# Seven Strassen products for half of each MLP up-projection chunk, interleaved with the down-projection of another chunk

## The reference, cut to what matters

```python
def squared_relu_mlp(u, w1, w2):
    hdn = jnp.square(jax.nn.relu(jnp.einsum("bsd,df->bsf", u, w1)))   # 256x2048 by 2048x8192
    return jnp.einsum("bsf,fd->bsd", hdn, w2)                          # 256x8192 by 8192x2048

for i in range(DEPTH):                                                 # DEPTH = 2
    u = rmsnorm(h, norm_mix[i])
    m = conformer_conv_module(u, ...) if i % 2 == 0 else short_gated_conv(u, ...)
    h = h + m
    h = h + squared_relu_mlp(rmsnorm(h, norm_mlp[i]), mlp_w1[i], mlp_w2[i])
    h = h + per_layer_embedding(h, p[i], norm_ple[i], ple_w_proj[i], ple_w_gate[i])
return rmsnorm(h, norm_final)
```

## Time and profile before

| what | value |
|---|---|
| median of three runs | 2257.17 us |
| span of the profiled execution | 2255.2 us |
| PE busy | 2239.5 us, 99% of the span |
| DVE busy | 1429.0 us, 63% |
| ACT busy | 1145.0 us, 51% |
| granted TensorE clock, mean | 0.999 |
| DMA read / written | 460.42 / 33.55 MB, 219 GB/s over the span |

### The profile page before, as it was taken

The page is one execution under the profiler, slowest core; times in us unless marked ns, Lnnn a source line. Parts: engine busy times, 40 slices in busy tenths (PEclk is TensorE's granted clock), DMA queues, the critical chain, the costliest instruction groups (busy, mean ns, idle before and its releaser), DMA issues.

```text
span 2255.2 us, 29901 instructions
## 1 busy us (share of the span) xinstructions
PE 2239.5 (99%) x10320; PEld 1867.2 (83%) x10320; DVE 1429.0 (63%) x1597; ACT 1145.0 (51%) x1424; POOL 157.0 (7%) x183
## 2 busy tenths in 40 slices
PE   9999999999999999999999999999999999999998
PEld 8998788888888888888888888888888888888886
DVE  6999876555545645566766667665455455555665
ACT  5666655534534534556644444554345345345555
POOL 3888000000000000000000000000000000000000
PEclk9999999999999999999999999999999999999999
DMA  9554577756756856877777677777567567667773
GB/s 343 163 161 139 163 235 252 243 188 214 251 188 196 266 190 203 254 218 261 217 241 223 214 246 216 255 240 244 193 200 260 196 200 256 199 209 220 267 242 112
DMA packets 494098, 494.86 MB, mean 219 GB/s; under 512 B 257936, under 2 KB 296016, under 8 KB 493264
## 3 DMA queue, kind: packets, MB, share of 16 engines
q1 hardware_dynamic: 492192, 491.31, 67.6%
q10 hardware_dynamic: 1696, 1.67, 0.2%
q0 software_dynamic: 144, 1.05, 0.1%
HBM read 460.42 MB, written 33.55 MB: 219 GB/s over the span
## 4 chain that ended last, share of the span: by engine, by line
PE 98%; DMA 1%; DVE 1%; ACT 0%; issue 0%; ACTq 0%; SPq 0%; DVEq 0%
PE acc L430 29%; PE acc L432 29%; PE acc L431 29%; PE acc L494 3%; PE acc L513 2%; PE acc L515 2%; PE acc L514 2%; PE acc L548 1%; PE acc L578 0%; PE acc L577 0%; PE acc L576 0%; DMA emb<-in_cf_b_pw 0%; DMA staged<-prows 0%; ACTq L720 0%; DMA pT<-staged 0%
## 5 line engine op out<-in xcount | busy, mean ns | idle before, releaser
L939 DVE TENSOR_TENSOR wlo<-raw,whi 128x1024 fp32r<-128x1024 f32 x728 | 880.8, 1222 | 591.0 <-ACT whi L598 587.2
L598 ACT ACTIVATE whi<-raw 128x1024 fp32r<-128x1024 f32 x728 | 762.0, 1057 | 775.6 <-PE acc L432 769.9
L430 PE MATMUL acc<-whi,b_hi 128*128 128x512 f32 x1632 | 635.4, 389 | 0.0
L432 PE MATMUL acc<-whi,b_lo 128*128 128x512 f32 x1632 | 634.9, 389 | 0.0
L431 PE MATMUL acc<-wlo,b_hi 128*128 128x512 f32 x1632 | 634.9, 389 | 0.0
L430 PE MATMUL acc<-whi,a_hi 128*128 128x512 f32 x1280 | 498.1, 389 | 0.3 <-DVE a_lo L1034 0.3
L432 PE MATMUL acc<-whi,a_lo 128*128 128x512 f32 x1280 | 497.9, 389 | 0.0
L431 PE MATMUL acc<-wlo,a_hi 128*128 128x512 f32 x1280 | 497.9, 389 | 0.0
L431 PEld LDWEIGHTS acc<-wlo,b_hi 128*128 128x128 f32 x1632 | 306.3, 188 | 63.9 <-issue 0.2
L430 PEld LDWEIGHTS acc<-whi,b_hi 128*128 128x128 f32 x1632 | 306.3, 188 | 63.8 <-DVE b_lo L1256 0.3
L432 PEld LDWEIGHTS acc<-whi,b_lo 128*128 128x128 f32 x1632 | 306.3, 188 | 63.8
(11 more groups left out here) (169 smaller groups left out, 1256.4 us busy)
## 6 DMA issues: line engine op xcount, KB each, us to landing
raw<-in_mlp_w SPq DMA_DIRECT2D x256, 1024.0 KB, 5.8
raw<-in_sc_w_in SPq DMA_DIRECT2D x48, 1024.0 KB, 6.7
raw<-in_cf_w_pw SPq DMA_DIRECT2D x64, 512.0 KB, 8.8
raw<-in_ple_w_gate SPq DMA_DIRECT2D x32, 1024.0 KB, 6.7
staged<-prows SPq DMA_DIRECT2D x240, 128.0 KB, 3.3
pT<-staged SPq DMA_DIRECT2D x56, 512.0 KB, 3.3
raw<-in_cf_w_pw SPq DMA_DIRECT2D x16, 1024.0 KB, 7.3
raw<-in_sc_w_out SPq DMA_DIRECT2D x16, 1024.0 KB, 7.5
```

What stands on the lines that cost most here:

```text
L430: nc.tensor.matmul(o, xhi[:, k, s], hi, start=first and c == 0, stop=False)
L432: mm = nc.tensor.matmul(o, xlo[:, k, s], hi, start=False, stop=last and c == 1)
L598: nc.scalar.activation(whi[:, e % SLOTS, :, :], raw[:, e // 2, 2 * (e % 2):2 * (e % 2) + 2, :], ACT.Copy).then_inc(hi_ready, 1)
L939: nc.vector.tensor_tensor(wlo[:, e % SLOTS, :, :], raw[:, e // 2, 2 * (e % 2):2 * (e % 2) + 2, :], whi[:, e % SLOTS, :, :].bitcast(F32), A ...
```

## The change: what it does

Tokens, input rows and output columns of an up-projection are cut in two. Of the 2048 input rows, the first 1024 are computed by Strassen's scheme: the 256 tokens are two halves of 128, the 1024 rows two halves of 512, and 1024 output columns (a *chunk* of the hidden width, two result blocks) two halves of 512. Seven products of 128 tokens by 512 rows by 512 columns take the place of eight. The other 1024 input rows are multiplied as before. A layer has eight chunks. The first is computed as two blocks in the old way; for the seven others there is a *step*, which also does the down-projection of the chunk before it.

A step is a list of 38 *slots* (`STEP`), each with one split of 128x1024 weights on ACT and DVE: 14 slots `m` (two for each of the seven products, 6 matmuls each), 16 slots `d` (down-projection of the former chunk, four for each 512 output columns, 12 matmuls each), and 8 slots `r` (the other 1024 input rows, 12 matmuls each). Slots 0 to 25 are `m` and `d` mixed (slots 0, 1, 2 are `m`, slot 3 `d`, then `m` and `d` by turns to slot 17), 26 to 33 are `r`, 34 to 37 `d`. The first down-projection columns, `("d", 0, ...)`, stand in slots 3, 5, 7 and 9, and the latter two of these need the second result block of the former chunk. After seven steps `END` does the down-projection of the last chunk in 18 slots, of which the first four are half as large.

- Weights of the products need differences of blocks: `weight_sum` on DVE, 8 in a step, in place in `raw`, two slots ahead of their use. On the token side four combinations `s_hi`, `s_lo` are made once for each layer (`combine`).
- The partial sums are combined in PSUM by ACT (two copies, L1002 and L1005 of the new kernel) and DVE (`mix`, four operations, ahead of slot 18).
- `raw` holds the four 1 MB fields of the Strassen weights; all other weights of a step come as 24 loads of 512 KB into a ring of four, `pl`, each issued when the piece four loads earlier has been split.
- The embedding `emb` is written to DRAM in the first mixer's output projection and read back at the end of each MLP, to make room.
- The ring of split weights keeps four places; the semaphores are now `slot_hi`, `slot_lo`, `slot_used`, with PE's increment at the end of every slot.

The core of the diff (the parts for SP, PE, ACT and DVE in this order):

```diff
+STEP = (("m", 1, 0), ("m", 1, 1), ("m", 5, 0), ("d", 0, 0), ("m", 5, 1), ("d", 0, 1),
+        ("m", 6, 0), ("d", 0, 2), ("m", 6, 1), ("d", 0, 3), ("m", 7, 0), ("d", 1, 0), ("m", 7, 1), ("d", 1, 1),
...
+END = (("d", 0, 0, 0), ("d", 0, 0, 1), ("d", 0, 1, 0), ("d", 0, 1, 1), ("d", 0, 2, None), ("d", 0, 3, None),
...
+SUMS = (5, 6, 7, 4)
+SUMMED = tuple(i for i, (kind, of, _) in enumerate(STEP) if kind == "m" and of in SUMS)
+FIELD = {1: 0, 5: 0, 6: 0, 4: 0, 7: 1, 3: 2, 2: 3}
+COMBO = {5: 0, 6: 1, 7: 2, 3: 3}
+BANK = {1: 0, 2: 0, 7: 1, 4: 1, 5: 2, 3: 2, 6: 3}
...
+FIELD_FREED = (at_slot("m", 4, 1), at_slot("m", 7, 1), at_slot("m", 3, 1), at_slot("m", 4, 1))
+HIDDEN_BEFORE = tuple(last_up(c) + SLOTS for c in range(2))
...
+            def load_step(layer, k, last=False):
+
+                r0, r1 = (Result(chunk(layer, k), c) for c in range(2))
+                for i in range(len(STEP)):
+                    free = low_done(layer, k, i)
+                    if i in PLAIN:
+                        n = PLAIN.index(i) + 4
+                        if n < LOADS:
+                            plain(layer, k, n, free)
+                        elif last:
+                            plain_end(layer, n - LOADS, free)
+                        else:
+                            plain(layer, k + 1, n - LOADS, free)
+                    if i == HIDDEN_BEFORE[0] - 1:
+                        stage_begin(r0.T)
+                    if i == HIDDEN_BEFORE[0]:
+                        stage_end(r0.T)
+                    freed = [f for f in (3, 2, 1, 0) if i == FIELD_FREED[f]]
+                    for f in () if last else freed:
+                        field(layer, k + 1, f, free if f == freed[0] else None)
+                stage_begin(r1.T)
+                stage_end(r1.T)
...
+            def multiply_step(layer, u, k, parity, first=False):
+
+                hid, base, n = X[1 - u], first_slot(layer, k), STEPS * layer + k
+                up, _, down = mlp[layer]
+                before = Result(up, 0) if first else Result(chunk(layer, k - 1), 0)
...
+                        if of == 2:
+                            pe.wait_ge(m1_copied, n + 1)
+                        if of == 4:
+                            pe.wait_ge(mixed, n + 1)
...
+                    if kind == "d" and of == 0 and part % 2 == 0:
+                        pe.wait_ge(operand_ready, 2 * before.o + part + 2)
+                    pe.wait_ge(slot_lo, base + i + 1)
+                    for m in range(1 if kind == "m" else 2):
+                        for c in range(2):
+                            if kind == "m":
+                                xhi, xlo = combination(u, of, 2 * part + c)
+                                mm = three(acc[:, BANK[of], :], xhi, xlo, ring(parity, i), c,
+                                           of in (1, 5, 6, 7) and part == 0 and c == 0,
+                                           of in (1, 5, 6, 7) and part == 1 and c == 1, of in (2, 3, 4))
...
+                    mm.then_inc(slot_used, 1)
...
+                up = mlp[layer][0]
+                multiply(up.b, up.a, 0, X[u], ready)
+                multiply(up.b + 1, up.a + 1, 1, X[u])
+                multiply_step(layer, u, 0, 0, True)
+                with pe.Fori(0, STEPS // 2) as it:
+                    multiply_step(layer, u, 2 * it + 1, 1)
+                    multiply_step(layer, u, 2 * it + 2, 0)
+                multiply_end(layer, u)
...
+                for i, (kind, of, part) in enumerate(STEP):
+                    if first and i == 3:
+                        process(Result(up, 1))
+                    if first and i == 8:
+                        operand_hi(Result(up, 1).x, 1, hid)
+                    if not first and i == 4:
+                        operand_hi(before.x, 2 * parity + 1, hid)
+                    if i == at_slot("m", 1, 1) + 5:
+                        act.wait_ge(slot_used, base + at_slot("m", 1, 1) + 1)
+                        nc.scalar.activation(m1_copy, acc[:, BANK[1], :], ACT.Copy).then_inc(m1_copied, 1)
+                    if i == at_slot("m", 5, 1) + 5:
+                        act.wait_ge(slot_used, base + at_slot("m", 5, 1) + 1)
+                        nc.scalar.activation(m5_copy, acc[:, BANK[5], :], ACT.Copy).then_inc(m5_copied, 1)
+                    for c in range(2):
+                        if i == HIDDEN_BEFORE[c]:
+                            act.wait_ge(slot_used, base + last_up(c) + 1)
+                            hidden(here[c], up_free)
+                    slot_split(layer, k, parity, i, product_source(n, i) if kind == "m" else plain_source(layer, k, PLAIN.index(i)))
+                operand_hi(here[0].x, 2 * (1 - parity), hid)
...
+            def run_end(layer, u):
+
+                hid, gain, down = X[1 - u], ROW_PLE + layer, mlp[layer][2]
+                before = Result(chunk(layer, STEPS - 1), 1)
+                for i, (_, j, part, single) in enumerate(END):
+                    if i == 4:
+                        operand_hi(before.x, 2 * (STEPS % 2) + 1, hid)
...
+            def weight_sum(n, i):
+
+                _, of, part = STEP[i]
+                b11, b12, b22, b21 = (raw[:, f, 2 * part:2 * part + 2, :] for f in range(4))
+                o, x, y, needs = {5: (b11, b12, b11, 1), 6: (b11, b22, b11, 2), 7: (b12, b22, b12, 2),
+                                  4: (b11, b21, b11, 3)}[of]
+                dve.wait_ge(field_ready[needs], 16 * n + 16)
+                nc.vector.tensor_tensor(o, x, y, ALU.subtract).then_inc(slot_sum, 1)
+
+            def mix(base, n):
+
+                b21, b12, b22 = acc[:, BANK[7], :], acc[:, BANK[5], :], acc[:, BANK[6], :]
+                dve.wait_ge(m1_copied, n + 1)
+                dve.wait_ge(slot_used, base + at_slot("m", 7, 1) + 1)
+                nc.vector.tensor_tensor(u2, b22, m1_copy, ALU.add).then_inc(u2_ready, 1)
+                dve.wait_ge(u2_ready, n + 1)
+                nc.vector.tensor_tensor(b21, b21, u2, ALU.add).then_inc(u3_ready, 1)
+                dve.wait_ge(u3_ready, n + 1)
+                dve.wait_ge(m5_copied, n + 1)
+                nc.vector.tensor_tensor(b22, b21, m5_copy, ALU.add)
+                nc.vector.tensor_tensor(b12, b12, u2, ALU.add).then_inc(mixed, 1)
...
+                for i, (kind, of, part) in enumerate(STEP):
+                    if first and i == 3:
+                        turn_hidden(Result(up, 1))
+                    if first and i == 8:
+                        operand_lo(Result(up, 1).xh, 1, hid)
+                    if not first and i == 4:
+                        add_down(layer, k - 1, 3)
+                    if not first and i == 6:
+                        operand_lo(before.xh, 2 * parity + 1, hid)
+                    for j, at in ((0, 14), (1, 22), (2, 29)):
+                        if i == at:
+                            if first and j == 0:
+                                dve.wait_ge(ss_ready, down.s)
+                            add_down(layer, k, j)
+                    if i == 18:
+                        mix(base, n)
+                    if i == HIDDEN_BEFORE[0]:
+                        turn_hidden(here[0])
+                    slot_low(layer, k, parity, i, raw[:, FIELD[of], 2 * part:2 * part + 2, :] if kind == "m" else
+                             pl[:, PLAIN.index(i) % 4, :, :])
+                    if i + 2 in SUMMED:
+                        weight_sum(n, i + 2)
+                operand_lo(here[0].xh, 2 * (1 - parity), hid)
+                turn_hidden(here[1])
...
+                def combine(e):
+                    if e == 1:
+                        dve.wait_ge(operand_ready, 2 * prev.o + 4)
...
+                        steps.mark(nc.vector.tensor_tensor(whole, X[u][0][:, 0:8, :].bitcast(F32),
+                                                           X[u][1][:, 0:8, :].bitcast(F32), ALU.add))
+                        steps.wait()
+                        a11, a12, a21, a22 = (whole[:, k:k + TILES, s:s + P] for s in (0, P) for k in (0, TILES))
+                        s1, s2, s3, s4 = (combos[:, i, :, :] for i in range(4))
+                        steps.mark(nc.vector.tensor_tensor(s1, a21, a22, ALU.add))
+                        nc.vector.tensor_tensor(s3, a11, a21, ALU.subtract)
+                        steps.wait()
+                        steps.mark(nc.vector.tensor_tensor(s2, s1, a11, ALU.subtract))
+                        steps.wait()
+                        nc.vector.tensor_tensor(s4, a12, s2, ALU.subtract).then_inc(combo_sum, 1)
+                    if e == 6:
+                        dve.wait_ge(combo_hi, layer + 1)
+                        nc.vector.tensor_tensor(s_lo[:, :, :, :], combos, s_hi[:, :, :, :].bitcast(F32), ALU.subtract
+                                                ).then_inc(combo_ready, 1)
```

469 lines of the change are left out of this document (351 added, 118 removed), and 7 rows, old and new, of tables (END, STEP).

## The result

The changed kernel takes 2354.43 us (median of 4 runs, 2351.74 to 2357.7), the one before 2257.15. The ratio is 1.043, with a 95% interval of 1.0417 to 1.0443. So it is 97 us slower. The forecast was 45 us slower, with a range that ended at 2338: the sign and the wait at slot 4 were right, but the size was less than half of what was measured, and a whole stage of waits was missed. The profiled execution has a span of 2355.9 us, 100.7 more than before.

What follows compares the result with a forecast made beforehand. PE, busy 99% of the span, was taken as the bound, each microsecond it waits costing a whole one. Waits of 82.5 us less 38.1 for removed matmuls gave +44.4, so 2302 us, range 2268 to 2338.

Steps and rivals of the forecast that it cites:

- 168 matmuls out, 38.1 us: Seven steps in each of two layers save 12 matmuls each, at 0.2266 us per matmul: 38.1 us less.
- The prices on DVE: Weight difference 1.16 us, `mix` 2.8 in all, DVE 67.5 of 84.3 us a step; `mix` and `pl` cost PE nothing.
- The exchange at slot 4: Second block's exchange outlasts PE's cover, 20.8 against 17.68 us: 3.15 at slot 4, 4.67 with slots 5 and 7, 12 steps.
- The restart behind a stop: After a wait, PE's cadence begins 0.3 us after DVE's end.
- The first step: First step of a layer: late field 1 and exchange stop PE at slots 1, 3 and 7, 8.0 us, twice.
- Rival 2: Exchange back before PE needs slot 4, DVE alone decides, 1.9 us a step: 2250 us; chance 6%.
- rival 3: Half of rival 2's case: exchange a microsecond or two shorter, 2270 to 2285 us; chance 9%.
- `END`, the step that failed: Last chunk's down-projection: same exchange wait ahead of its slot 4, cover 16.32 us, 4.74 us, twice.
- the entry to the gate's blocks: Result 2's exchange ends at 16.7 us against 16.32 of cover: 0.5 us, twice.
- Rival 1: PE's clock falls to half speed in the new waits, +36 us, 2338; 15% together with a slow exchange.
- The exchange's length: From SP's first issue to usable `pT`, 8.93 us, taken from the trace.
- The estimate by the Trainium skill: By its DMA page the exchange would be some 1.2 us shorter and the time about 2283; not adopted.

Runs made afterwards that it cites:

- run 8: run 3 plus Experiment 5's order in `END`, and fields 1 and 2 of a layer's first step loaded ahead of the `combo_ready` wait: 2274.29 us.
- Experiment 2: Changed kernel with DVE turning a chunk's second block ahead of slot 37's low part, not behind it and the first block's operand: 2338.67 us.
- Experiment 5: run 3 with DVE in `END` adding and turning result j+1 ahead of the low operand of result j: 2283.17 us.
- experiment 9: run 8 with `END` reordered: second result's first pieces mixed in, second block's operand needed at the sixth piece, results added at slots 11, 14, 17: 2270.38 us.
- run 10: Kernel before, without Strassen products, both operand parts of each exchanged hidden block made ahead of half 5 of the next block, not behind half 7: 2416.44 us.
- run 11: Kernel before, without Strassen products, both operand parts of each exchanged hidden block made ahead of half 4 of the next block, not behind half 7: 2532.15 us.
- run 3: Changed kernel with Experiment 2's earlier turn and ACT's high operand of the second block ahead of slot 6's split, not slot 4's: 2293.16 us.
- run 4: Changed kernel with each weight difference on DVE working on two columns in place of 1024: 2353.75 us.

## Why the prediction was wrong in size, by its own steps

- **168 matmuls out, 38.1 us**: right. 10152 are left, and outside of stops and half clock they keep the old spacing.
- **The prices on DVE**: right. A difference takes 1219 ns (1206 to 1241 in 112), back to back 1.14 us from start to start. `mix` and the small ring `pl` cost nothing: no PE wait stands at slots 18 and 19, and ACT's 86.7 us behind `pl`'s loads seem to reach no PE wait (in run 8 they are 85.4, and the steps have next to no stops).
- **The exchange at slot 4**: right in chain and nearly in size. 3.15 us were forecast there; it is 2.0 to 2.6 us of idle time and 0.30 around it in eleven of the steps, 3.72 in one, whose exchange took 10.4 us. The exchange begins 9.2 us behind the end of slot 33 on the mean, where 8.33 had been worked out. Slot 5 has 0.4 to 0.6 in nine of the steps (0.96 forecast with its seam), slot 7 at most 0.2 (0.56). What was missed are the stops at slots 0, 1 and 3, 0.15 to 0.6 us each: the prediction counted the turn and operand at the end of a step against the exchange, not against the low parts of slots 0 to 3 behind them on DVE. Experiment 2 took nearly all of them away. Together it is 6.0 us a step, where 4.67 were forecast.
- **The restart behind a stop.** The prediction read 2087.69 in the earlier trace rows as the start of the second matmul. It is the end of the first, from which the chain goes on; the second starts at 2087.53. So the cadence is back 0.15 us behind DVE's end and not 0.3, and each stop was priced some 0.15 too high, far too little to matter for the miss.
- **The first step**, 8.0: right in size, wrong in its parts. The stops are 4.1 and 4.4 us at slot 1 (3.2 forecast with its seam), 1.0 at slot 3 (2.8) and 1.5 and 1.6 at slot 7 (2.0). Half clock behind the one at slot 1 comes on top.
- **Rival 2** (the exchange is in time) and **rival 3** (half of it) had 15% and are wrong.
- **`END`, the step that failed.** It was priced at its slot 4 alone, 4.74 (5.76 and 4.49 of idle time measured). The prediction then priced "the entry to the gate's blocks" at 0.5, with the exchange of a result at 16.7 against 16.32 of cover, and took all the results of `END` before it as hidden. It asked for the cover of one exchange and not what is queued behind what. On DVE result j+1 is added only behind the operand of result j, so that a period of 16.7 us stands against 10.9 of cover. It cost 25.2 us in `END` and 10.8 at the gate and behind it, where 1.0 had been set down. Experiment 5 shows that the order on DVE had a part in it (10 us in the medians, with half clock). How the rest is shared between the exchange's length, lengthened by weight loads around it, and SP's wait for the former one stays open; experiment 9 shows that wait at work in two of three distances.
- **The clock, a rival of its own that should have been a term.** Rival 1 gave it 15%, as a case in which all the stops are followed by half clock. It came together with the forecast's stops, not in place of them: 20.8 us, and some 26 with the ends of the slow stretches. Only 6 of the 12 stops at slot 4 were followed by it, but all eight stops from 3.6 us up in this kernel. The Trainium skill (TensorE: Matmul & The Clock Gate, Part 1) has a fall to 1.2 GHz behind an idle stretch as a rule; the trace agrees with its direction, and where its rule for kernels goes by the idle stretch's length, the runs show stops of the same length with and without it (3.26 and 3.35 us above).
- **The exchange's length.** 9.24 us in the step shown, where 8.93 had been taken; 11.0 in `END` (1033.66 to ACT's read at 1044.65), where SP took 3.77 us to issue four DMAs. The estimate by the Trainium skill (DMA: Bandwidth & Descriptors, "Anatomy of one DMA"), an exchange 1.2 us shorter and a time of 2283, is further off than the one by rows.

Added up: 44.4 forecast, 35.0 for the rest of `END` and the gate (25.2 + 10.8 - 1.0), 14.1 in the intervals between slots 4, 6.4 in the starts, 1.8 ahead: 101.7, against 100.7 measured. The clock's share is spread over these and is no further term.

## What to carry to other kernels

A place where a wait is added has to be asked for its period as well as for its first cover: if the list of an engine puts the operand of one result ahead of the adding of the next, the exchange's latency becomes the distance between results. Where PE was never idle, each new stop costs more than its length (here 0.30 us, and 1.7 to 2.4 us more where the clock falls: 2.0 us besides the idle time in run 10, 2.2 in the changed kernel, 2.7 in run 11), so price it as a sum and not as a rival. And before work is taken off a busy engine, look at what it waits for: removing 112 us of DVE's work brought nothing while PE still waited for the exchange, moving one ACT instruction by two places brought 37 us. Last, a transfer that starts earlier is not back as much earlier: 3.7 us became 2.2 in run 2.

## What the runs showed of the hardware that was not expected

- PE's clock falls to half behind some stops of 2 us and not behind others of 3.5 us (3.47 in run 10, 3.58 in run 3). Of stops from 1.9 us up, half clock followed behind 14 of 22 in the changed kernel (by way of a short stop in between in three cases), 21 of 22 in run 4, 24 of 32 of 2.7 to 4.7 us in run 10, and 32 of 32 of 5.4 to 6.3 us in run 11. What decides it for the shorter ones stays open. It lasts for 13 matmuls at most.
- A stop at full clock costs 0.30 us besides its idle time (the mean of 49 in the changed kernel, of 10 in run 3 and of 8 in run 10). The last matmul before it ends 0.16 us behind the cadence, the first matmul behind it takes 0.50 us, and the next starts 0.34 behind it, where 0.39 and 0.227 are usual:

```profile
785.76 0.50 PE L430 MATMUL acc<-whi,a_hi 128*128 128x512 f32 x1 [3.26 <-DVE wlo L941]
786.10 0.39 PE L431 MATMUL acc<-wlo,a_hi 128*128 128x512 f32 x1
786.33 0.39 PE L432 MATMUL acc<-whi,a_lo 128*128 128x512 f32 x1
```

- The same four DMAs of an exchange take SP 3.0 us to issue in most places (the medians of all runs are 2.98 to 3.14) and up to 7.93 in run 5 and 8.45 in run 8, in both with four weight loads issued in the seven us ahead of them.
